# Two-layer block in float32: six of eight convolution blocks as quarter-width matmuls, second memory's projections as split products

## What is computed

```python
def conformer_conv(xn, pw1_w, pw1_b, dw_w, dw_b, ln_g, ln_b, pw2_w, pw2_b):
    a, g = jnp.split(xn @ pw1_w + pw1_b, 2, axis=-1)
    h = a * jax.nn.sigmoid(g)
    h = depthwise_conv(h, dw_w) + dw_b          # 31 taps over positions, each channel by itself
    h = jax.nn.silu(layernorm(h, ln_g, ln_b))
    return h @ pw2_w + pw2_b
# cross_attn of the same layer: k, v = split(rmsnorm(mem, norm_mem) @ wkv, 2)
```

## Time and profile before

| | |
|---|---|
| median of 3 runs | 2198.6 us (2196.98 to 2199.11) |
| span of the profiled execution | 2198.1 us |
| its own time | only its span is given: 2198.1 us |
| PE busy | 2158.0 us, 98% |
| DVE busy | 1727.4 us, 79% |
| ACT busy | 1360.8 us, 62% |
| mean DMA rate | 281 GB/s |
| stage of the change | from 444 us to 536 us after the span's start |

### The profile page before, as it was taken

How to read it: one execution, slowest core, us unless ns; L and a number is a source line. 1 busy time by engine, 2 the same in 40 slices (tenths; PEclk the granted TensorE clock), 3 DMA queues, 4 the chain that set the end, 5 groups by cost and what they waited for, 6 DMA issues and landing times. The chain is left out here.

```text
span 2198.1 us, 30267 instructions
## 1 busy us (share of the span) xinstructions
PE 2158.0 (98%) x11668; PEld 1850.8 (84%) x11668; DVE 1727.4 (79%) x1615; ACT 1360.8 (62%) x1208; POOL 82.4 (4%) x79
## 2 busy tenths in 40 slices
PE   8999999999999999999999999999999999999997
PEld 8998999877888888888888888888889888888886
DVE  5765555798678888888888888889866664798887
ACT  5444333526467777777777777777756344577775
POOL 1010000000000000000000000000000000000000
PEclk9999999999999999999999999999999999999999
DMA  8462555632379999999999999999944163699995
GB/s 318 166 178 96 191 197 185 213 112 82 131 258 387 381 388 372 380 376 376 381 373 383 367 388 364 393 370 386 377 139 169 67 223 116 203 382 380 382 376 224
DMA packets 275864, 617.26 MB, mean 281 GB/s; under 512 B 9552, under 2 KB 36384, under 8 KB 275776
## 3 DMA queue, kind: packets, MB, share of 16 engines
q1 hardware_dynamic: 266688, 584.43, 72.6%
q0 software_dynamic: 9088, 31.60, 4.8%
HBM read 603.41 MB, written 12.58 MB: 280 GB/s over the span
## 5 line engine op out<-in xcount | busy, mean ns | idle before, releaser
L2541 DVE TENSOR_TENSOR w_low<-ring,w_high 128x2048 fp32r<-128x2048 f32 x426 | 971.4, 2290 | 130.1 <-ACT w_high L1756 129.0
L1756 ACT ACTIVATE w_high<-ring 128x2048 fp32r<-128x2048 f32 x426 | 815.3, 1917 | 166.9 <-PE ps L819 166.9
L818 PE MATMUL ps<-w_high,parts 128*128 128x512 f32 (+2 forms) x1896 | 735.0, 388 | 0.0
L817 PE MATMUL ps<-w_high,parts 128*128 128x512 f32 x1560 | 616.9, 395 | 1.6 <-DVE parts L2249 1.4
L819 PE MATMUL ps<-w_low,parts 128*128 128x512 f32 x1560 | 608.5, 390 | 0.0
L818 PEld LDWEIGHTS ps<-w_high,parts 128*128 128x128 f32 x1896 | 356.6, 188 | 69.1
L817 PEld LDWEIGHTS ps<-w_high,parts 128*128 128x128 f32 x1560 | 293.1, 188 | 64.0 <-issue 5.9
L819 PEld LDWEIGHTS ps<-w_low,parts 128*128 128x128 f32 x1560 | 292.8, 188 | 62.7
L1955 DVE TENSOR_TENSOR w_low<-ring,w_high 128x2048 fp32r<-128x2048 f32 (+2 forms) x117 | 262.2, 2253 | 99.4 <-ACT w_high L1469 98.4
L1469 ACT ACTIVATE w_high<-ring 128x2048 fp32r<-128x2048 f32 (+2 forms) x117 | 219.7, 1883 | 132.3 <-PE ps L819 120.1
L817 PE MATMUL ps<-XT_high,w_high 128*128 128x256 f32 x1024 | 292.5, 286 | 3.4 <-DVE parts L1946 1.6
(11 more groups left out here) (448 smaller groups left out, 1620.8 us busy)
## 6 DMA issues: line engine op xcount, KB each, us to landing
ring<-in_od_moe_gu SPq DMA_DIRECT2D x224, 1024.0 KB, 8.2
ring<-in_od_moe_down SPq DMA_DIRECT2D x112, 1024.0 KB, 7.6
ring<-in_w SPq DMA_DIRECT2D x96, 1024.0 KB, 8.4
ring<-in_ev_ffn_gu SPq DMA_DIRECT2D x22, 1024.0 KB, 7.4
ring<-in_xa_wkv SPq DMA_DIRECT2D x8, 2048.0 KB, 8.6
ring<-in_od_pw_w SPq DMA_DIRECT2D x6, 2048.0 KB, 8.4
ring<-in_w_in SPq DMA_DIRECT2D x6, 2048.0 KB, 8.5
ring<-in_ev_ffn_down SPq DMA_DIRECT2D x11, 1024.0 KB, 5.1
```

The source lines that it names most:

```text
L817: mm(out_, xh, wh, start=start, stop=False)
L818: mm(out_, xl, wh, start=False, stop=False)
L1756: A(w_high[:, j % SPLITS, :], ring[:, j % NS, :], ACT.Copy).then_inc(moe_sem(k, "high"), 1)
L2541: V.tensor_tensor(w_low[:, j % SPLITS, :], ring[:, j % NS, :], w_high[:, j % SPLITS, :].bitcast(F32), SUB)\
```

## The change

1. The convolution's blocks 2 to 7 run on PE, blocks 0 and 1 on DVE. The 128 channels of a block are four groups of 32. For each group, four DMAs of 36 KB put its 32 channels four times onto the 128 partitions, each time moved on by one position (`shifted`). A stationary matrix of 128 rows and 32 columns then takes four taps at once; 8 steps give all 31. The four groups of a step are four matmuls that write four different quarters of the partitions of one PSUM bank, `tile_position=(0, 32 * g)`. That makes 32 float32 matmuls of 256 columns for a block, 192 in all.
2. The shifted copies are 96 DMAs within the on-chip memory, 32 partitions by 284 float32 each: 32 for blocks 2 and 3 on SP ahead of the load of Bv0, 32 for blocks 4 and 5 on SP ahead of the load of pw2_0, 32 for blocks 6 and 7 on POOL.
3. DVE builds the stationary matrices of a block with one multiplication of 128x1024 (`build_taps`) from a table of taps that the host arranges and one DMA loads; the 62 diagonals on ACT and the three loads of the vector table are gone.
4. Bk0, Bk1, Bv0, Bv1 become split products. Bv0 and Bv1 move behind the convolution (the matrices lie where the values go). The filler transposes are gone.
5. The sum over channels is made by seven additions on DVE and one matmul instead of a reduction and three matmuls; all squares are on ACT, DVE adds them to two blocks, and two matmuls replace eight.
6. The place of a split half is numbered from the first expert mixture on, so that the numbering fits with eight more halves.

```diff
-TAPS_ON_PE = 2
-DIAGONALS = 16
-EARLY_TAPS = 5
+SHIFTS = 4
+GROUPS_OF_32 = 4
+STEPS = 8
+DVE_BLOCKS = 2
+SHIFTED = 256 + SHIFTS * (STEPS - 1)
...
+        def shift_copies(eng, blocks):
+            for b in blocks:
+                for g in range(GROUPS_OF_32):
+                    for s in range(SHIFTS):
+                        eng.dma_start(shifted(b, g)[s * 32:(s + 1) * 32, :], HC[g * 32:(g + 1) * 32, b, s:s + SHIFTED])\
+                            .then_inc(S(f"shifted{b // 2}"), 16)
...
             for i in range(n_dense):
+                if i == unit_panel[UNIT["Bv0"]]:
+                    sync.wait_ge(S("xs_ready"), 3)
+                    shift_copies(sync, (2, 3))
+                if i == unit_panel[UNIT["pw2_0"]]:
+                    sync.wait_ge(S("glu"), 2)
+                    shift_copies(sync, (4, 5))
                 load(i, i >= SLOTS)
...
             memory(5, "mem")
+            pool.wait_ge(S("glu"), 2)
+            shift_copies(pool, (6, 7))
...
-            for b in range(TAPS_ON_PE):
-                for k in range(CONV):
...
-                    pe.wait_ge(S("diagonal_ready"), i + 1)
-                    mm(ps[:, 4 + b, 0:T], w_(10240, DIAGONALS, P)[:, i % DIAGONALS, :], HC[:, KC - TAPS_ON_PE + b, k:k + T],
-                       start=(k == 0), stop=(k == CONV - 1)).then_inc(S("diagonal_used"), 1)
...
-            keep_busy(16, 4)
...
+            for n in range(KC - DVE_BLOCKS):
+                b = n + DVE_BLOCKS
+                pe.wait_ge(S("taps_built"), n + 1)
+                pe.wait_ge(S(f"shifted{b // 2}"), 16 * 2 * SHIFTS * GROUPS_OF_32)
+                if n >= 3:
+                    pe.wait_ge(S("features_by_act"), n - 2)
+                for i in range(STEPS):
+                    for g in range(GROUPS_OF_32):
+                        last = mm(ps[32 * g:32 * g + 32, 4 + n % 3, n // 3 * T:n // 3 * T + T], TAPS[n % 2][:, i * GROUPS_OF_32 + g, :],
+                                  shifted(b, g)[:, SHIFTS * i:SHIFTS * i + T], start=(i == 0), stop=(i == STEPS - 1),
+                                  tile_position=(0, 32 * g))
+                last.then_inc(S("features_made"), 1)
+            project("Bv0", halves=(0,))
+            pe.wait_ge(S("sums_built"), 2)
+            mm(ps[:, 7, 0:T], ONES, CHANNEL_SUM, start=True, stop=True).then_inc(S("sums_ready"), 1)
+            project("Bv0", halves=(1,))
+            pe.wait_ge(S("sums_built"), 3)
+            mm(ps[:, 7, T:2 * T], ONES, SQ[:, 0, :], start=True, stop=False)
+            mm(ps[:, 7, T:2 * T], ONES, SQ[:, 1, :], start=False, stop=True).then_inc(S("sums_ready"), 1)
+            project("Bv1")
...
-            project("Bv1", tcs=(1,))
             project("pw2_0", first=True)
```

```diff
+                    step(V.tensor_reduce(MASK, IDENT.rearrange("p (j c) -> p c j", c=32), X, ADD))
+                    dve.wait_ge(S("vectors_loaded"), 16 * VEC_LOADS)
+                    taps(0, 5)
+                    lows(halves_to("Bk0"))
+                    taps(5, 8)
+                    columns_low(("xa_norm_mem", 8))
                 unit_ready(dve, u)
...
+            lows(halves_to("Bk1"))
+            taps(8, 16)
+            build_taps(0)
+            build_taps(1)
+            lows(halves_to("Bv0"))
+            for n in range(2, KC - DVE_BLOCKS):
+                taps(3 * n + 10, 3 * n + 13)
+                build_taps(n)
+            taps(28, CONV)
+            step(V.tensor_tensor(CHANNEL_SUM, CO[:, 0, :], CO[:, 1, :], ADD))
+            for b in range(2, KC):
+                if b == KC - 1:
+                    lows(halves_to("Bv1", -1))
+                dve.wait_ge(S("features_by_act"), b - 1)
+                add = V.tensor_tensor(CHANNEL_SUM, CHANNEL_SUM, CO[:, b, :], ADD)
```

More of the change, by code:

```diff
@@ L643, in _, with project @@
             seen = {"act": 0, "vector": 0}
-            def project(name, first=False, halves=(0, 1), tcs=(0, 1)):
+            def project(name, first=False, halves=(0, 1)):
                 u = UNIT[name]
                 _, _, _, n, columns, src = UNITS[u]
-                x, pair = sources[src], PAIRS[u % 2]
+                pair = PAIRS[u % 2]
                 if u >= 2:
                     pe.wait_ge(S(f"unit_read{u % 2}"), u // 2)
[L652 to L670, removed]
+                project_parts(u, columns, n, pair, first, halves)
             def turn_half(half, src=H, shift=0):
@@ L759, in project_parts, with turn @@
                     last.then_inc(S("parts_read"), 1)
-            def turn(src, ready, n, parts=True):
+            def turn(src, ready, n):
                 pe.wait_ge(S(ready), n)
@@ L821, in memory_projections @@
             def memory_projections(tag, ready, value):
-                turn(XS, ready, value, parts=(tag != "B"))
+                turn(XS, ready, value)
                 if tag == "A":
@@ L1427, in rms @@
                 root()
-            def columns(dst, gain, banks=(4, 5)):
-                n_["turn"] += 1
-                act.wait_ge(S("turned"), 4 * n_["turn"] - 2)
-                for kc in range(4):
-                    src = ps[:, 4 + kc // 2, kc % 2 * T:kc % 2 * T + T]
-                    if gain is None:
-                        last = A(dst[:, kc, :], src, ACT.Copy)
-                    else:
-                        last = A(dst[:, kc, :], src, ACT.Copy, scale=vec(gain[0], gain[1] + kc))
-                    if kc % 2:
-                        last.then_inc(S("columns_by_act"), 1)
             def columns_high(gain, half=None, shift=0, free=None):
@@ L1525, in memory_projections @@
                             A(XT_high[:, 2 * i:2 * i + 2, :], w_(10240, KC, T)[:, 2 * i:2 * i + 2, :], ACT.Copy).then_inc(S("columns_by_act"), 1)
-                    if tag == "B" and j == 0:
-                        for i in range(DIAGONALS):
-                            diagonal(i)
-                    if tag == "B" and j == 1:
-                        highs(halves_to("pw2_1", -1))
                     if tag == "C" and j == 1:
@@ L1763, in experts @@
                     q = split_at[UNIT["fqk"]]
[L1764 removed]
+                    act.wait_ge(moe_sem(k, "read"), turns * N + (1 + split_slot(q - N)))
                     highs(q + 1)
@@ L2304, in _ @@
                 else:
-                    for k in range(EARLY_TAPS):
-                        for kc in range(4):
-                            last = tap(kc, k)
-                        step(last)
+                    step(V.tensor_reduce(MASK, IDENT.rearrange("p (j c) -> p c j", c=32), X, ADD))
[4 more added lines that the diff above has]
+                    columns_low(("xa_norm_mem", 8))
                 unit_ready(dve, u)
@@ L2322, in _ @@
                     lows(halves_to("value1"))
-            columns(XT, ("xa_norm_mem", 8))
-            for k in range(CONV):
-                for kc in range(KC - TAPS_ON_PE):
-                    if kc >= 4:
-                        last = tap(kc, k)
-                    elif k + EARLY_TAPS < CONV:
-                        last = tap(kc, k + EARLY_TAPS)
-                step(last)
-            V.tensor_reduce(VAR, CO[:, 0:6, :].rearrange("p k t -> p t k"), X, ADD).then_inc(S("features_by_vector"), 1)
-            lows(halves_to("pw2_0", -1))
+            lows(halves_to("Bk1"))
[13 more added lines that the diff above has]
+                add = V.tensor_tensor(CHANNEL_SUM, CHANNEL_SUM, CO[:, b, :], ADD)
+                if b < KC - 1:
+                    step(add)
+            add.then_inc(S("sums_built"), 1)
             dve.wait_ge(S("sums_ready"), 2)
```

195 lines of the change are left out of this document (102 added, 93 removed).

## The result

| | before | after |
|---|---|---|
| median of all runs | 2198.2 us (2196.98 to 2199.11, 4 runs) | 2176.0 us (2174.55 to 2178.22, 4 runs) |
| ratio | | 0.9901, interval 0.9887 to 0.9915 |
| span of the profiled execution | 2198.1 us | 2172.7 us, in a run of 2174.55 us |
| transposes of the memory start | 443.82 us | 443.06 us |
| pw2_0 starts | 536.20 us | 514.03 us |

The account below looks back on a forecast made before the run. The prediction took PE as the bound with DVE balanced against it; pw2_0 starting at 515.1 instead of 536.2 us saves 21.1 us, 2198.1 to 2177.0, stated as 2178; likeliest case 2174 to 2187, 8-in-10 range 2173 to 2200.

Parts of the forecast that it names:

- Keys: Key products on PE: 192 fast matmuls take 23.0 us against 28.1, after a 0.6 us wait for the memory's low columns.
- The convolution: 192 quarter-width matmuls on PE: four at once, 20.8 us, 3.5 us a block; bound if each runs alone, 83.3 us.
- Emptying the array: PE before and after the narrow matmuls: 0.6 us added, bounds 0 and 2.
- DVE's pace: DVE during the convolution: three tap pairs and a build, 3.9 us a block; last build ends at 485.8 us.
- Behind the convolution: PE from the convolution's end to pw2_0, with values, sums and waits: 24.1 us; DVE and ACT's chain within 1 us.
- Edits at zero: Tap loads, fewer transposes, extra halves on ACT and DVE, renumbered places: together between -0.5 and +0.5 us.
- The shifted copies: Copies issued 0.5 us apart on SP and 0.52 on POOL: price zero, cover 8 us on SP.
- rival 2: Copies late: above 0.75 us an issue on SP, blocks 4 and 5 wait; at 1.0 us, time 2194 us; chance 0.12.
- its two cases: Cases counted as faster: the forecast with its own range, 0.52, and late copies, 0.12, the latter not in full.
- Two at once: Convolution on PE: strict start order lets two matmuls overlap, 41.7 us, 6.9 a block, time 2198.0 us; chance 0.20.
- One after the other: Convolution on PE: quarters do not overlap, 83.3 us, 13.9 a block, time 2239 us; chance 0.13.
- A bound elsewhere: Channel sum or SiLU chain late by a few us: 2180 to 2186 us; chance included in the forecast's 0.52.

Follow-up runs that it names:

- two other orders of DVE's work: Changed kernel with six early taps moved behind the gated unit: 2175.4 us; that plus two, not three, tap pairs ahead of builds 2 to 5: 2176.1 us.
- runs of four: Changed kernel with the block's matmuls reordered, four steps of one quarter in a row before the next quarter: 2198.4 us, ratio 1.0004.
- run of eight: Changed kernel with the block's matmuls reordered, all eight steps of one quarter before the next quarter: 2218.6 us, ratio 1.0093.
- the run with PE's half: Changed kernel without the last four of eight convolution steps on PE: 2173.5 us, ratio 0.9889.

## Why the prediction was right, and where its steps were off

The forecast was 2178 us, the time is 2176.0 us. Of the forecast's cases the first held, and step by step:

- **Keys.** 64 split products at 0.12 us a matmul: forecast 23.0 us, measured 23.3 us. The wait before them was priced at 0.6 us, and is 1.2 us; neither of the two other orders of DVE's work got it back.
- **The convolution.** Forecast 3.5 us a block and an end near 490 us, measured 3.45 us and 490.4 us. (Its own terms, 469.2 + 20.8, give 490.0; the sum goes on from 490.4.) The lower end was chosen with nothing in the trace that showed matmuls side by side, for the reason that the four share neither columns, partitions nor results. This reason is not enough: in the runs of four and eight steps the quarters share as little, and a block takes 7.1 and 10.5 us. That the change's program happens to alternate between the quarters after every matmul is what the forecast needed and doesn't name as a condition; in that it was lucky. An estimate from the Trainium skill's 2.38x for three column tiles (TensorE: Matmul & The Clock Gate, Part 3), scaled to four, is 26 us. The trace has 20.9 us, a full fourfold, which the Trainium skill gives as the upper limit (TensorEngine Tiling (Array Packing), Theoretical Speedup).
- **Emptying the array.** Priced at 0.6 us. From the last full-width record to the first narrow one are 0.21 us, where fast matmuls stand 0.12 us apart, and behind the stretch the first record starts 0.33 us after the last narrow ones: about 0.2 us in all. That this is the emptying of the array, no run shows.
- **DVE's pace.** Forecast 3.9 us a block and the last build at 485.8 us; measured 3.88 and 486.2 us. Channel sum ready at 495.4 us by forecast (its terms add up to 493.7), 494.2 us measured. PE asks for it at 496.0 us, so the spare is 1.7 us there and 0.6 us at the last build; "within 1 us" was a little too close.
- **Behind the convolution.** Forecast 24.1 us and 0.6 for the array, measured 23.7 us for both. From the memory's transposes to pw2_0: 71.3 us forecast, 71.0 us measured.
- **Edits at zero.** The rows of the memory's transposes start between 442.95 and 443.44 us in the kernels with the change and at 443.82, 443.32 and 443.23 us in three executions with the convolution of before: on average 0.3 us earlier, in the bounds given, though single executions are up to 0.9 us apart.
- **The shifted copies, the term that was mis-sized.** The step "SP's issues stand 0.5 us apart" was taken from loads and carried over to copies of 32 partitions. They take 0.68 to 0.74 us, and `glu` 2, which lets the second set begin, comes at 451.2 us instead of 450.1. The second set is issued until 474.0 us instead of 466, and has landed by about 475 to 476 us instead of 468. The price stayed zero, but the "cover 8 us" was 0.6 to 1.6 us, and the limit of rival 2, 0.75 us an issue, was almost reached. A chance of 0.12 for it was too small for what the rows could show.
- **The span and the median.** I took the median to be 0.5 us over the profiled span. A run's time is 1.8 us above its own span (2174.55 and 2172.7, 2198.6 and 2196.8), so the profiled execution of before took about 2199.9 us by this difference (an estimate), over its median and not under it. In spans, the saving was forecast at 21.1 us and shown as 24.1 to 25.4 us, of which 22.05 us are the stage's, in medians as 22.2 us.
- **The chances.** Faster was given 0.65, but its two cases add up to 0.64, and part of one was to be left out.

**The rivals.** *Two at once* falls by the starts of four records within 0.02 us. It rested on starts that never leave the program's order. The Trainium skill states this as a rule (TensorE: Matmul & The Clock Gate, Part 3). Between quarters this case's trace doesn't agree: in the run of eight a record of the next quarter starts at 480.28 us, ahead of one at 480.93 us that stands before it in the program, and the measurement decides. Its number did come up: in the order with runs of four the time is 2198.4 us, where it said 2198.0, but by a block of 7.1 us that comes from the short reach and not from this rule; that is chance. *Copies late* did not occur, though its mechanism is shown by the run with all copies on SP, where the lower clock behind the wait adds to it. *One after the other* falls: even in runs of eight a block takes 10.5 us and not 13.9. *A bound elsewhere* stays a near miss: 0.5 us at the channel sum once the blocks are earlier.

Why the gain is no larger than 1% is also answered. The convolution on PE costs 20.9 us for six blocks where it cost 26.8 us for two, and the rest of the gain is in the products around it. Little more is to be had from either engine alone: with PE's share halved DVE's builds and its channel sum hold the stage after 1.6 us, with DVE's share halved PE does.

## What to carry to other kernels

Quarter-width matmuls gave a true fourfold here when the program alternated between the quarters at least every four records (two float32 matmuls). Runs of eight records left 1.9-fold and runs of sixteen 1.3-fold, and the kernel's gain was gone with either; lengths between four and eight were not tried. Many small copies are priced by their issue, and the price hangs on the queue and the shape: here 0.6 to 0.7 us on SP and 0.5 us on POOL. Take it from a row of the same shape, or keep both ends in the range, and divide the copies over two queues. A wait of PE can cost more than its length: behind 12.45 us of waiting, 2.7 us of work were done at the lower clock. Where two engines are balanced to within 2 us, test by halving each and both: three numbers say more than the order of any chain.

## What the runs showed of the hardware that was not expected

- The reach between quarters: matmuls of another quarter start when at most about four records of the busy one are outstanding. Blocks of 3.45, 3.45, 7.14 and 10.48 us with runs of 2 (one step), 4, 8 and 16 records.
- Starts leave the program's order between quarters: at 480.28 us, in the run of eight, a record starts ahead of three that stand before it.
- TensorE's granted clock fell to 0.50 in the middle of a wait of 12.45 us, and behind three waits of 1.6 to 1.95 us in the run with PE's half; the page's slices of 54 us show neither.
- The narrow weight loads take 0.11 us (0.19 us for those of 128 columns) and are hidden: the steps stand 0.216 us apart like the records of full width, though all four quarters use the same rows of the array. One of PEld's groups in the stretch:

```profile
L1046 PEld LDWEIGHTS ps<-work 128*32 128x32 f32 x160 | 7.6, 110 | 2.7
```

- A 36 KB copy within the on-chip memory costs SP's queue 0.62 to 0.74 us and POOL's 0.49 us to issue. Their loads take both about 0.5 us, so an issue's price on SP could not be carried over from one to the other.
